# A three-block network on one Trainium2 core: the weight buffers moved by 128 bytes

## The reference

```python
h2 = modulate(rms_norm(x, g_norm2[l]), shift2, scale2)
u = causal_depthwise_conv(h2 @ w_up[l], w_conv[l], b_conv[l])      # 1024 -> 5632
val, gte = jnp.split(u, 2, axis=-1)
x = x + (1 + gate2[:, None, :]) * ((val * jax.nn.silu(gte)) @ w_down[l])   # 2816 -> 1024
...
def swiglu(h, w_gu, w_down):                                         # twice more
    gate, up = jnp.split(h @ w_gu, 2, axis=-1)
    return (jax.nn.silu(gate) * up) @ w_down
```

## The kernel before

| tiles | start above a multiple of 256 |
|---|---|
| `raw0` to `raw3` | 192 |
| `whi0`, `whi1`, `whi2` | 192 |
| `wlo0` | 0 |
| `wlo1`, `wlo2` | 192 |
| `X`, `ub`, `rs_t`, `ssb`, `adac`, `masks`, `one` | 192 |
| `h_hi`, `h_lo`, `m_hi`, `m_lo`, `mm_*`, `kb_*`, `c_*` | 0 |

## Time and profile before

### The profile page before, as it was taken

How to read it: one execution, slowest core, us unless ns; L and a number is a source line. 1 busy time by engine, 2 the same in 40 slices (tenths; PEclk the granted TensorE clock), 3 DMA queues, 4 the chain that set the end, 5 groups by cost and what they waited for, 6 DMA issues and landing times.

```text
span 1065.0 us, 22984 instructions
## 1 busy us (share of the span) xinstructions
PE 1030.9 (97%) x10004; PEld 976.9 (92%) x10004; DVE 733.2 (69%) x1194; ACT 562.0 (53%) x858; POOL 0.9 (0%) x7
## 2 busy tenths in 40 slices
PE   7999999999999999998999999999999999999996
PEld 6898888999999998887879999999998799999996
DVE  3897658899976667887547655666757755665654
ACT  4456374665655548754236444454667655444541
POOL 0000000000000000000000000000000000000000
PEclk8999999999999999999999999999999999999999
DMA  9977545466645553331004555456323445554551
GB/s 348 399 258 306 184 173 209 174 227 248 228 149 188 202 228 119 120 121 42 4 2 162 197 197 195 140 191 215 112 75 127 175 154 182 180 193 162 175 180 40
DMA packets 31236, 185.82 MB, mean 174 GB/s; under 512 B 3472, under 2 KB 4768, under 8 KB 13984
## 3 DMA queue, kind: packets, MB, share of 16 engines
q1 hardware_dynamic: 31136, 184.36, 48.6%
HBM read 183.29 MB, written 1.05 MB: 173 GB/s over the span
## 4 chain that ended last, share of the span: by engine, by line
PE 85%; DVE 6%; ACT 3%; DMA 3%; issue 2%; SPq 1%; DVEq 0%; ACTq 0%
PE banks L382 46%; PE banks L1385 17%; PE banks L347 3%; PE banks L379 2%; PE banks L659 2%; DVE wlo L327 1%; DMA land<-in_mkv_a 1%; PE banks L1928 1%; PE banks L1569 1%; ACT whi L312 1%; PE banks L1918 1%; DMA raw<-in_a_in 1%; PE banks L594 1%; DVE adac L578 1%; PE banks L662 1%
## 5 line engine op out<-in xcount | busy, mean ns | idle before, releaser
L327 DVE TENSOR_TENSOR wlo<-raw,whi 128x2048 fp32r<-128x2048 f32 (+3 forms) x163 | 323.0, 1982 | 167.5 <-ACT whi L312 167.0
L312 ACT ACTIVATE whi<-raw 128x2048 fp32r<-128x2048 f32 (+3 forms) x163 | 270.3, 1661 | 105.8 <-PE banks L1385 73.0
L382 PE MATMUL banks<-h_hi,wlo 128*128 128x256 f32 x1376 | 176.2, 280 | 0.0
L382 PE MATMUL banks<-h_lo,whi 128*128 128x256 f32 x1376 | 175.7, 279 | 0.0
L382 PE MATMUL banks<-h_hi,whi 128*128 128x256 f32 x1360 | 174.3, 280 | 0.1
L382 PEld LDWEIGHTS banks<-h_hi,wlo 128*128 128x128 f32 x1376 | 166.6, 188 | 1.5 <-issue 1.2
L382 PEld LDWEIGHTS banks<-h_lo,whi 128*128 128x128 f32 x1376 | 164.7, 187 | 3.1 <-issue 2.6
L382 PEld LDWEIGHTS banks<-h_hi,whi 128*128 128x128 f32 x1360 | 164.1, 188 | 2.3 <-issue 1.2
L1411 ACT ACTIVATE u<-u 128x256 f32<-128x256 f32 x44 | 18.4, 418 | 124.9 <-DVE u L1465 124.9
L1385 PE MATMUL banks<-m_hi,wlo 128*128 128x256 f32 x528 | 74.0, 279 | 0.0
L1385 PE MATMUL banks<-m_lo,whi 128*128 128x256 f32 x528 | 73.3, 277 | 0.0
(11 more groups left out here) (453 smaller groups left out, 1414.7 us busy)
## 6 DMA issues: line engine op xcount, KB each, us to landing
raw<-in_ada SPq DMA_DIRECT2D x24, 1024.0 KB, 6.2
raw<-in_w_up SPq DMA_DIRECT2D x22, 1024.0 KB, 4.8
raw<-in_a_gu SPq DMA_DIRECT2D x22, 1024.0 KB, 4.8
raw<-in_b_gu SPq DMA_DIRECT2D x22, 1024.0 KB, 4.9
raw<-in_w_in SPq DMA_DIRECT2D x12, 1024.0 KB, 5.9
raw<-in_w_down SPq DMA_DIRECT2D x16, 704.0 KB, 4.1
raw<-in_a_in SPq DMA_DIRECT2D x11, 1024.0 KB, 4.9
raw<-in_a_down SPq DMA_DIRECT2D x16, 704.0 KB, 4.1
```

Source lines behind the costliest of these rows:

```text
L312: act.activation(hi_s[k % NSPLIT][:, 0:w], raw[n % NRAW][:, 0:w], ACT.Copy).then_inc(*hi_made.tick(k))
L327: dve.tensor_tensor(lo_s[s][:, 0:w], raw[n % NRAW][:, 0:w], hi_s[s][:, 0:w].bitcast(F), SUB).then_inc(*lo_made.tick(k))
L382: i_ = pe.matmul(b[0:m, j * T:(j + 1) * T], a[:, kt * step + j * m:kt * step + j * m + m], x[:, kt, :], start=st, stop=sp)
```

## The change

No instruction is added, removed or moved. Only the sizes of pads change, and with them the addresses of tiles.

```diff
         raw = [sb(f"raw{i}", [P, SLOT]) for i in range(NRAW)]
+        sb("pad_low", [P, 32])
         split = []
-        for i, n in enumerate((0, 0, 0, 16, 48, 0)):
+        for i, n in enumerate((0, 0, 0, 32, 32, 0)):
             if n:
                 sb(f"pad_w{i}", [P, n])
             split.append(sb(f"whi{i}" if i < NSPLIT else f"wlo{i - NSPLIT}", [P, SLOT], R))
...
-        sb("pad_mid", [P, 40])
+        sb("pad_mid", [P, 8])
```

## The result

| | before | after |
|---|---|---|
| median | 1064.03 us (1062.46 to 1067.45, 10 executions) | 1061.72 us (1060.16 to 1064.11, 10 executions) |
| ratio | | 0.9971 (95% interval 0.9957 to 0.9985) |
| span of the profiled execution | 1065.0 us | 1062.3 us |
| TensorE busy | 1030.9 us | 1025.1 us |

The change gains 0.29% by the ratio.

The account below looks back on a forecast made before the run. TensorE, busy in 97% of the span and holding 85% of the last-ending chain, was taken as the bound. Odd passes -3.0 and broken stages -1.6 sum to -4.6 us, giving 1060.0 us, range 1057 to 1078.

Parts of the forecast that it names:

- The kind of change: Whole kernel: no instruction is touched, so only the pace of instructions can change; chance of a faster kernel 0.45.
- The odd pass: Feed-forward passes out of `wlo0`: 510 matmuls go from 120 ns to the pace of their neighbours, -3.0 us.
- The broken stages: Stages outside the feed-forward networks: a quarter of 1592 matmuls goes from slow to fast, -1.6 us, bounds 0 and 3.5.
- the state: TensorE streams persist fast or slow: feed-forward matmuls all fast would be 8.6 us less, all slow 12.3 us more.
- four exchanged passes: Preview with weight buffers as moving operand, loaded one at 0: two of four fast, so fast entries look likelier.
- The pull: `wlo0` passes in slow streams: a `wlo0` at 192 among buffers at 64 makes them fast about as often as now.
- The sum: Whole kernel: -3.0 - 1.6 = -4.6 us, span 1065.0 to 1060.4, median 1064.58 to 1060.0 us.
- Only TensorE's pace reaches the end: Whole kernel: TensorE is busy in 97% of the span; copies, DMAs and other tiles were taken as zero.
- Rival 1: Feed-forward streams: the jump does not pull, slow entries stay slow until the next break; 1077.4 or 1072 us; chance 0.31.
- Rival 2: Each break draws the pace, half the streams entered fast, no pull; 1064.8 us, spread 1060 to 1070; chance 0.24.
- Rival 3: Whole kernel: addresses do not count, the paces have another cause that stays; 1064.6 us; chance 0.03.
- What would show it: Signs in the trace: low passes of 11 at 1.25 us, feed-forward windows at most 115.0, broken-stage windows 0.5 us shorter, copies unchanged.

Follow-up runs that it names:

- others_192: Changed kernel with X, ub, rs_t, ssb, adac, masks and one back at 192, weights unchanged: 1060.19 us, ratio 0.9950 to the kernel before.
- all_64: Changed kernel with wlo0 at 64 like the five other weight buffers: 1065.36 us, ratio 0.9981 to the kernel before.
- all_192: Kernel before with wlo0 at 192 like the other weight buffers: 1078.76 us, ratio 1.0105 to the kernel before.
- after_again: The changed kernel itself, unaltered, measured once more: 1061.27 us, ratio 0.9962 to the kernel before.
- lows_192: Changed kernel with all three low-weight buffers at 192, the high ones at 64: 1061.13 us, ratio 0.9944 to the kernel before.
- mixed: Changed kernel with whi0, whi2, wlo1 at 192 and whi1, wlo0, wlo2 at 64: 1059.71 us, ratio 0.9945 to the kernel before.
- all_128: Changed kernel with all six weight buffers 128 above a multiple of 256: 1084.42 us, ratio 1.0159 to the kernel before.

## Why the prediction was right, and where by luck

- **The kind of change: right.** Only TensorE's pace changed; the copies stayed at 1983 and 1663 ns, and the small tiles carry none of it (others_192).
- **The odd pass, -3.0 us: right.** The 525 distances out of `wlo0` in the feed-forward networks fell from 119.86 to 114.97 ns, 2.6 us.
- **The broken stages, -1.6 us: the mechanism was right, the size too small.** They gave 0.9 + 3.0 = 3.9 us. The 0.9 is the odd pass in these stages, which the prediction left out; the 3.0 is the state, within the bound of 3.5. 1144 of some 2050 distances are fast there, 309 before: the quarter that I took from four exchanged passes was two fifths. That entries are fast more often at 64 than at 192 is shown by all_64 against all_192 (971 against 199).
- **The pull, "about as often as now": wrong in this step.** It works wherever the `wlo0` pass is 16 long, five times of five in the first up projection. In the down projections, where `wlo0` at the moving tile's place pulled in the kernel before, it no longer does: two of three were entered slow and stayed slow. The rest of the feed-forward networks became 1.7 us slower, where I had zero; in after_again, where no down projection was slow, it is 1.6 us faster than before. The prediction weighed the jump and the place but not the length of the pass at it, nor what stands ahead of the pass.
- **The sum.** -2.6 + 1.7 - 3.9 = -4.8 us in the streams against a forecast of -4.6: the failed pull (+1.7) and what the broken stages gave beyond the forecast (-2.3) nearly cancel. That is luck: in after_again, with the down projections entered fast, the same terms are -3.1 - 1.6 - 3.7 = -8.4 us, and the span there is 1060.6.
- **"Only TensorE's pace reaches the end": wrong for two stages.** The forecast put the whole sum on the span. The copies had been priced as covered by 5.4 us of TensorE, each by itself and by a mean over chunks of several widths (1661 and 1982 ns; a chunk of an up projection takes 1.91 and 2.29 us). But ScalarE's copy, VectorE's difference and the operations of the gate hang on one another, and their round of 5.59 us is longer than 5.44. The wait for `m_hi` took 1.9 us back, the wait for `S` in the first block was 1.2 us longer, and the span fell by 2.7. With the streams' -4.8 these make -1.7; the remaining 1.0 us I cannot place. Neither it nor the 1.2 need be the change's: the wait for `S` lies between 1.2 and 4.1 us over all the runs, and the stretch between the first network and the second was some 2 us shorter in this execution than in five others (190.0 to 190.9). The round as the bound is read from the chain (TensorE's 90.6% of it in that stage gave way to the copies' 74.6%) and borne out by the other kernels: all_64, lows_192, others_192 and mixed, fast in the second and third up projection, have the `m_hi` wait of 1.7 to 1.9 us; the kernel before and all_192 do not have it. No run made the round shorter, which would have shown it directly.
- **The rivals.** Rival 1 is true of another layout (all_192) and false of this one. Rival 2's draw is real in two places: wherever there is no jump (all_64), and near the start of the down projections, where it made 4.1 us between two executions of one program. Rival 3 is excluded by all_192 and all_128, which are 1.0% and 1.6% slower with not one instruction changed.
- **The page SBUF — State Buffer of the Trainium skill**, section "SBUF: two separate sides": that TensorE never waits on another engine there, no run here contradicts. But TensorE's pace does depend on where its own two tiles lie to one another: 113.3 or 117.8 ns at 64 and 192, 118.7 at 128, 120.0 at the same place.
- **What would show it.** First up projection's window 115.64 us for 999 matmuls against "at or below 115.0": missed by its slow stretches, the other two, 114.62 and 113.76, met it. Third chunk of the ring ends the slow stretch: yes, 270.25. First pass behind the breaks: 2.13, still the slow entry. Low passes of 11 at 1.25 us from start to start: yes in the fast second down projection, but about 1.30 in the two that stayed slow. L383's windows of the broken stages "shorter by 0.5 us each": 69.35 to 69.09, 70.13 to 68.80 and 65.64 to 65.67 (with 534 matmuls, not 528), so met by one of three, or two if the last is taken by matmul. The copies: unchanged.

## What to carry to other kernels

When a profile shows equal instructions at two or three sharp paces, divide pass lengths by counts and ask which operands lie where before looking for a wait; a pad of 128 bytes is then an experiment that costs next to nothing, and all tiles at one place is the control. In this kernel it paid to put at least one weight buffer of a ring at another place than its neighbours, better one in each chunk, since a settled slow stream was left only by a jump or at the next break or stall. And when the busiest engine gains in a stage, even the 1% of the third up projection here, add up the round of the engines behind it: 5.59 us stood against TensorE's 5.54 before and 5.44 at the fast pace.

## What was not expected of the hardware

- **The paces have a common measure.** The slow pace is a cycle of three distances with a sum of 353.3 ns (118, 118, 117), the fast one repeats 113.33 ns (114, 113, 113), the third is 120.0, or a cycle of five with a sum of 600 (120, 121, 124, 117, 118). All are multiples of 6.67 ns: 53, 17, 18 and 90. In fast streams the starts keep nearly one phase modulo 6.67 ns over a stage, across breaks too. The slow cycle has three matmuls; 16 and 13 leave a rest of 1 over threes, 12 none, 11 a rest of 2. This fits the rows of the table behind a jump, not the two runs of 11 behind a break, and no run tested it.
- **One direction only.** Fast streams were never thrown out by a jump (0 of 903), slow ones were pulled out only on the way back (57 of 95, none of the 89 on the way there).
- **A distance of 128 bytes has a pace of its own.** 1.90 / 16 = 118.7 ns, between the slow pace and the 120.0 of the moving tile's own place; it is a cycle of five distances with a sum of 593.3 ns, 89 times 6.67. It persists like the others and has a slower neighbour, 120.0, in which the whole second network went. No stream of all_128 was fast: 1.6% on the whole kernel.
- **Entries vary.** The down projections of one unchanged program are entered at either pace in different executions; what decides it at a stall stays open.
